# Nine token tiles regrouped from 3-3-3 to 2-3-4 in a fused encoder layer, with smaller rings beside them

## The reference

```python
h  = modulate(x, sh1, sc1)                       # layer norm, scale and shift from silu(c) @ w_ada
gq, gk, gv, glr, gog, sq, sk, sv, mg_a, mg_b = split_cols(h @ w_in)
# branch A: gated linear attention, 4 heads (dk 128, dv 256): S_t = diag(a_t) S_{t-1} + k_t v_t^T ; o_t = q_t S_t
branch_a = (rms_norm(o_gla) * gla_norm_w * silu(gog)) @ w_gla_proj
# branch B: stick breaking, 16 heads of 64: A[t,s] = sigmoid(z_ts) * prod_{s<j<t} (1 - sigmoid(z_tj))
branch_b = o_sb @ w_sb_proj
mix = (sigmoid(mg_a) * branch_a + sigmoid(mg_b) * branch_b) @ w_o
x   = layer_norm(DN_ALPHA * x + g1 * mix, ln1_w, ln1_b)
h2  = modulate(x, sh2, sc2)
# PEER: 8 heads; the 16 best of 128 keys on each of two sides, then the 16 best of their 256 sums
act = gelu(einsum('nhkd,nd->nhk', peer_u[eid], h2))      # 128 experts for each token
f   = einsum('nhk,nhkd->nd', softmax(top) * act, peer_v[eid])
x   = layer_norm(DN_ALPHA * x + g2 * f, ln2_w, ln2_b)
```

## Time and profile before

| | |
|---|---|
| runs shown | 4612.33, 4616.6, 4627.35 us |
| median | 4616.6 us |
| span of the profiled execution, first to last instruction | 4610.3 us |
| the median beside this span | 6.3 us more |
| busy PE, DVE, ACT, POOL | 76%, 59%, 20%, 53% of the span |
| moved by DMA | 1572.17 MB, 341 GB/s in the mean |

### The profile page before, as it was taken

The page is one execution under the profiler, slowest core; times in us unless marked ns, Lnnn a source line. Parts: engine busy times, 40 slices in busy tenths (PEclk is TensorE's granted clock), DMA queues, the critical chain, the costliest instruction groups (busy, mean ns, idle before and its releaser), DMA issues.

```text
span 4610.3 us, 46291 instructions
## 1 busy us (share of the span) xinstructions
PE 3486.6 (76%) x16122; PEld 1731.9 (38%) x16122; DVE 2734.5 (59%) x6463; ACT 911.3 (20%) x1858; POOL 2441.7 (53%) x2375
## 2 busy tenths in 40 slices
PE   7989999989899898978898988998443344433456
PEld 4656755655356443544443554434100000000011
DVE  3443412788876768775568757777843565575410
ACT  3552310134423100133444222001000000000000
POOL 0000000275777565567776766655666666666665
PEclk9999999999999899999999988998655555555567
DMA  7774452799999999999998999999999899999998
GB/s 305 285 263 191 163 164 82 277 328 329 347 377 374 384 419 400 407 351 378 391 387 321 375 358 406 407 403 393 374 378 379 336 372 377 374 370 352 375 372 316
DMA packets 422693, 1572.17 MB, mean 341 GB/s; under 512 B 47720, under 2 KB 63464, under 8 KB 411328
## 3 DMA queue, kind: packets, MB, share of 16 engines
q0 software_dynamic: 340384, 1289.90, 72.2%
q1 hardware_dynamic: 78448, 271.38, 15.8%
q10 hardware_dynamic: 3632, 7.94, 0.5%
HBM read 1526.42 MB, written 42.61 MB: 340 GB/s over the span
## 4 chain that ended last, share of the span: by engine, by line
PE 42%; DVE 18%; POOL 11%; another core or an unknown queue 10%; issue 9%; DMA 8%; ACT 1%; ACTq 0%; DVEq 0%; SPq 0%; POOLq 0%
PE bank L2606 7%; DVE peer_u_ring L2712 6%; PE wide L1891 6%; DMA peer_v_ring<-in_peer_v,expertsT 5%; POOL peer_u_ring L2539 4%; PE wide L1460 4%; PE wide L808 4%; POOL peer_v_ring L2549 4%; PE wide L2233 4%; PE wide L1448 3%; PE wide L871 2%; POOL w_ring L2549 2%; DMA peer_u_ring<-in_peer_u,experts 2%; PE wide L881 2%
## 5 line engine op out<-in xcount | busy, mean ns | idle before, releaser
L2539 POOL DMA_INDIRECT peer_u_ring<-in_peer_u,experts x1098 | 1153.2, 1050 | 603.0 <-issue 299.5
L2549 POOL DMA_INDIRECT peer_v_ring<-in_peer_v,expertsT x840 | 881.9, 1050 | 515.1 <-PE bank L2606 222.6
L2712 DVE SCALAR_TENSOR_TENSOR peer_u_ring<-peer_u_ring,wide 128x1024 f32<-128x1024 f32 x654 | 781.7, 1217 | 408.0 <-DMA peer_u_ring<-in_peer_u,experts 325.8
L2606 PE MATMUL bank<-peer_v_ring,peer_lone 128*32 128x512 f32 x3360 | 607.6, 730 | 450.3 <-DMA peer_v_ring<-in_peer_v,expertsT 280.9
L2606 PE MATMUL bank<-w_ring,peer_lone 128*32 128x512 f32 x1056 | 303.5, 962 | 345.7 <-DMA w_ring<-in_peer_v,expertsT 199.5
L2712 DVE SCALAR_TENSOR_TENSOR peer_u_ring<-peer_u_ring,peer_h 128x1024 f32<-128x1024 f32 x444 | 532.4, 1219 | 15.0 <-DMA peer_u_ring<-in_peer_u,experts 9.9
L2606 PEld LDWEIGHTS bank<-peer_v_ring,peer_lone 128*32 128x32 f32 x3360 | 92.8, 117 | 791.3 <-issue 771.9
L2549 POOL DMA_INDIRECT w_ring<-in_peer_v,expertsT x264 | 252.3, 956 | 141.2 <-issue 74.6
L808 PE MATMUL wide<-hT,w_ring 128*128 128x384 f32 x768 | 271.5, 501 | 6.9 <-ACT hT L589 3.6
L2606 PEld LDWEIGHTS bank<-w_ring,peer_lone 128*32 128x32 f32 x1056 | 50.5, 140 | 582.0 <-issue 576.6
L1460 PE MATMUL wide<-w_ring,hT 128*128 128x256 f32 x1152 | 260.4, 383 | 0.2 <-issue 0.2
(11 more groups left out here) (332 smaller groups left out, 5204.5 us busy)
## 6 DMA issues: line engine op xcount, KB each, us to landing
w_ring<-in_weights SPq DMA_DIRECT2D x312, 512.0 KB
sb_kc<-in_kcT POOLq DMA_DIRECT2D x16, 2048.0 KB, 7.7
sb_vc<-in_vc POOLq DMA_DIRECT2D x16, 2048.0 KB, 8.6
peer_u_ring<-in_peer_u,experts POOLq DMA_INDIRECT x1098
mod_w<-in_w_ada SPq DMA_DIRECT2D x15, 1024.0 KB, 10.8
peer_v_ring<-in_peer_v,expertsT POOLq DMA_INDIRECT x840
mod_w_later<-in_w_ada SPq DMA_DIRECT2D x9, 1024.0 KB, 7.0
scores<-sel_sc SPq DMA_DIRECT2D x6, 1024.0 KB
```

Of the source, the lines that this page charges most:

```text
L2539: pool.indirect_dma_start(buffer, None, K.A["peer_u"], bass.IndirectOffsetOnAxis(ap=K.ids_of[:, j % CHOSEN, k:k + 1], axis=0)).then_inc(lo ...
L2549: pool.indirect_dma_start(buffer, None, K.A["peer_v"], bass.IndirectOffsetOnAxis(ap=K.ids_of_turned[:, j % CHOSEN, t:t + 1], axis=0)).then ...
L2606: last = pe.matmul(self.F.psum[strip:strip + 32, :], self.lone[:, mark - at:mark - at + 32], self.buffer("v", m)[0][:, c * HALF:(c + 1) * ...
L2712: dve.scalar_tensor_tensor(u, u, 1.0, h2, ALU.mult, ALU.mult, accum_out=self.dots[:, j % 2, k:k + 1]).then_inc(self.dot_done, 1)
```

## The change

The groups become {0, samples}, {1, 2, 3}, {4, 5, 6, 7}. The u ring has six buffers instead of eight, there are two places for the chosen lists instead of four and one for the gates, and the buffers of the stages are laid out anew so that a group of four tiles fits. The first group has one prompt tile, so its stick stage has one key step per pair instead of two, and the order in `tensor_early`, `scalar_early` and `vector_early` loses the second step's calls. New waits guard the places that are used sooner again. The turned outputs of the GLA stage have two buffers only where they fit (first group); the banks of the selection follow the number of tiles. The causal masks of prompt and samples are two tensors now.

```diff
-NU, NV = 8, 6
+NU, NV = 6, 6
-CHOSEN = 4
+CHOSEN = 2
-GROUPS = grouped(((0, 2, True), (2, 5, False), (5, 8, False)))
+GROUPS = grouped(((0, 1, True), (1, 4, False), (4, 8, False)))
...
-            i, u = 2 * p, 2 * p
+            u = 2 * p
             self.c_scores(pe, G, u)
...
-            self.to_here(pe, G, i)
+            self.to_here(pe, G, p)
...
-            self.later_keys(pe, G, i)
-            self.scores(pe, G, i + 1)
             next(ahead, None)
-            self.values(pe, G, i)
+            self.values(pe, G, p)
             self.c_scores(pe, G, u + 1)
             next(ahead, None)
             self.c_turn(pe, G, u)
-            self.to_here(pe, G, i + 1)
...
+    def turned_slots(self, G):
+
+        return 2 if 2 * G.T <= max(g.T for g in GROUPS) else 1
...
-                if n == 0 and h >= 2:
-                    act.wait_ge(self.oT_out[h % 2], 16 * (2 * G.n + h // 2))
+                was = h - self.turned_slots(G)
+                if n == 0 and was >= 0:
+                    act.wait_ge(self.oT_out[was % 2], 16 * (2 * G.n + was // 2 + 1))
...
+        if j:
+            dve.wait_ge(self.K.peer.w_ready, j)
+        gates = self.K.gates[:, :].rearrange("p (h k) -> p h k", h=PEER_HEADS)
...
-    REFILL, MORE_FROM = 16, 5
-    TURN = SLOTS % (NU + NV)
+    REFILL, MORE_FROM = 16, 4
+    TURN = -SLOTS % NU
...
     def free_ids(self, dve, j):
         if j >= CHOSEN:
-            dve.wait_ge(self.v_used, P // 2 * (j - CHOSEN + 1))
+            dve.wait_ge(self.dot_done, SLOTS * (j - CHOSEN + 1))
```

More of the change, by code:

```diff
@@ L870, in to_here @@
             clears = kb == G.hi - 1 and (h == 0 or G.W > HALF // 2)
-            last = pe.matmul(r[:, h, c0:G.W], K.from_here[:, :], self.l[:, n % self.NL, h, c0:G.W], start=clears, stop=True, skip_group_check=True)
+            last = pe.matmul(r[:, h, c0:G.W], K.from_here[:, :], self.l[G.n][:, n % self.NL, h, c0:G.W], start=clears, stop=True, skip_group_check=True)
         last.then_inc(self.R.full, 1)
@@ L880, in later_keys @@
             for h in range(2):
-                last = pe.matmul(r[:, h, c0:G.W], K.before[:, :], self.l[:, n % self.NL, h, c0:G.W], start=False, stop=True, skip_group_check=True)
+                last = pe.matmul(r[:, h, c0:G.W], K.before[:, :], self.l[G.n][:, n % self.NL, h, c0:G.W], start=False, stop=True, skip_group_check=True)
             last.then_inc(self.l_used, 1)
@@ L1008, in tensor_early @@
             self.c_turn(pe, G, u)
-            self.to_here(pe, G, i + 1)
             next(ahead, None)
-            self.later_keys(pe, G, i + 1)
             self.c_values(pe, G, u)
-            next(ahead, None)
-            self.values(pe, G, i + 1)
             next(ahead, None)
@@ L1599, in key_scales @@
         m = self.prompt_tile(G, h, n)
-        if h or n >= 2:
-            at = self.tile(G, h, n - 2) if n >= 2 else self.tile(G, h - 1, G.np + n - 2)
+        had = h * G.np + n - 2
+        if had >= 0:
+            at = self.tile(G, *divmod(had, G.np))
             act.wait_ge(self.att_bank(at).full, self.att_bank(at).full_at["att", at])
@@ L1736, in hide_future @@
             dve.wait_ge(self.O.full, self.O.full_at["o", tile - 2])
-        dve.tensor_tensor(self.att[:, tile % 2, :], out[:, 0:P], self.K.causal[:, int(n == G.np), :], ALU.mult).then_inc(bank.kept, 1)
+        dve.tensor_tensor(self.att[:, tile % 2, :], out[:, 0:P], (self.K.causal_sample if n == G.np else self.K.causal)[:, :], ALU.mult).then_inc(bank.kept, 1)
     def next_state(self, dve, G, h, n):
@@ L1897, in scalar @@
         K = self.K
-        act.wait_ge(K.gla.oT_out[0], 16 * 2 * (G.n + 1))
+        for n in range(2):
+            act.wait_ge(K.gla.oT_out[n], 16 * 2 * (G.n + 1))
         for j in range(KC):
```

108 lines of the change are left out of this document (58 added, 50 removed).

## The result

| | before | after |
|---|---|---|
| median, us | 4619.65 (4 runs, 4612.33 to 4627.35) | 4871.35 (4 runs, 4864.29 to 4874.12) |
| profiled execution, span | 4610.3 | 4868.8 |
| ratio | | 1.053, interval 1.0498 to 1.0561 |

The changed kernel is slower by 5.3%. The forecast was 4830, in a range of 4715 to 4930.

A forecast was written before the change was run, and what follows sets the result against it. PE was taken to bound the middle, with DMA a close second, and gathers the tail. Front 726, second group 890, third 1505 and tail 1707 sum to 4828 us; with 6 carried over, rounded down, 4830, range 4715 to 4930.

The forecast's parts named there:

- its main term: Tail after the last stages: 530 dots instead of 402.5, 1707 us with the drain instead of 1345, so +362 us.
- That bytes do not bound the middle: Second and third groups' stages: PE is the floor, needing 1009 and 1224 us without value-row waits; DMA a close second.
- The tail is limited by the gathers: Tail: the gathers, not the choice of the next tile, limit it; a dot with its two gathers takes 2.84 us.
- A faster tail: Rival, in the tail: POOL's pace allows 2.49 us a slot, tail 190 us shorter, total 4640 us; chance 5%.
- (b) Rings: u ring of six instead of eight, POOL still six ahead: costs 0 us, ends -5 and +60.
- (c) Lists and single buffers: New waits name work 12 to 100 slots earlier: 0, ends 0 and +10; single turned GLA buffer 0, up to +5 a head.
- Front: First group's stages, 3 tiles to 2: 192 us less, ending at 726 us instead of 918.
- Second and third group, 890 and 1505: Lengths of the two later groups' stages: 890 us instead of 1073, and 1505 us instead of 1274.
- The ring starves both sides: Rival: PE stays at 88% in the middle (+137 us), a tail slot takes 3.0 us (+85), about 5050; chance 8%.
- DMA stays full, the shorter front is the gain: Rival: after the front the rings keep DMA full, so the end moves with the front to 4418 us; chance 4%.

The follow-up runs named there:

- 3-3-3: The kernel before the change, its tiles in three groups of three, with eight u buffers: 4619.65 us; with six u buffers instead, 4716.05 us.
- the runs with half rows: Each value gather brings 256 KB instead of 512, PE's work kept: 4598.18 us in the kernel before, 4843.58 us in the changed kernel.
- 2-3-4: The changed kernel's grouping, two, three and four tiles: 4871.35 us with six u buffers; 4791.64 us with eight, some small loads left out.
- the three runs: Changed kernel, front's stick stage: useless PE products added, 4834.21 us; sample pass's DVE scan cut to 64 columns, 4830.45 us; cache loads halved, 4835.58 us.

## Why the prediction was right, and where it was not

**The total and its main term: right.** The tail's 402.5 dots became 529, as forecast (530), for +383 us against +362. The slot is 2.885 instead of 2.84 us. The ring seems to have its part in these 0.045 us: in 3-3-3 the step from eight buffers to six made the tail 16 us longer, and in the changed kernel with eight a slot is again 1510 us / 530 dots = 2.85.

**That bytes do not bound the middle: right,** by the runs with half rows. That PE's own work is its floor fits, but was not shown. The worth that I gave to PE's waits for value rows was too high: 58 us of them went with half rows, and the middle was 6 us shorter.

**"The tail is limited by the gathers", with a slot set by DMA: right number, wrong limit.** In the rival *A faster tail* I wrote that it "would need the DMA to do better". With 25% fewer bytes to move the tail was no faster. POOL's pace plus its stalls is the limit as far as the profile shows, and the 2.49 us that I gave for POOL leaves the stalls out: they are 94 us in 402.5 slots, 0.23 us each, and the waits for dots are another 0.13, which with 2.49 make 2.85. The term came out right because the slot was measured and carried over, not derived.

**(b) Rings, "I take 0": the failed step.** Measured were 96 us in 3-3-3 and 40 to 70 in 2-3-4, about the upper end of 60 that I kept for it. The argument was that POOL needs 2.49 us a slot where 2.84 and more pass, so it catches up. But with six buffers POOL stood 218 us for dots in the third group of 3-3-3 where it had stood 89, and PE 100 us for values where it had waited 50. The reading that I give to this is that in the middle the dots do not come evenly, since DVE serves the stages too, and that POOL's one queue carries u and v gathers, so a wait for a dot holds values back as well. Averages over a slot do not see that. The other half of the argument, that longer slots make six buffers reach as far as seven, fits the smaller cost in 2-3-4, but no run tests it by itself.

**(c) Lists and single buffers, "0":** not tested alone. In the trace of the changed kernel the write that the single turned buffer could hold up (`gla_oT`, L1658) shows waits for PE only, 15.4 and 23.2 us in the two later groups, so nothing speaks against it.

**Front: mis-sized by 28 us, with the wrong reason.** The front ended at 754 us for 726. Merge (-47 for -52), output projection (-15 for -17) and norm (-2 for -3) held. GLA gave 71 instead of 57. The selection gave 7 instead of 15: at its end PE stands 19.2 us for the next group's norm on DVE, which is busy with the choice of the heads. Stick gave 22 instead of 48. I cut its gain for the sake of the cache loads, and these had air. As the three runs read, the removed key step had been cover for the sample pass's chain on ACT and DVE, and with PE waiting for that chain the granted clock is 0.83 where it was 0.95.

**Second and third group, 890 and 1505: met by two errors that cancel.** That is luck. The changed kernel with eight buffers, which is what these terms reckoned, shows 876 and 1460. Its idle times are 61 and 106 us, as predicted (57 and 110). PE's work is 815 and 1354 instead of 833 and 1395. I had carried over busy times of a middle at clock 0.94, and here it is 0.96 and 0.97. Taken at these clocks, my 833 and 1395 would be 816 and 1352, so this is about the whole difference. The ring then put back what the work had been overrated by. I had said that PE's waits for value rows would nearly vanish in the middle. In the third group 42.5 us stayed, and with eight buffers 21.8.

**The rivals.** *The ring starves both sides* was named and priced at 5050, but I gave it as all or nothing. The truth lies between: the ring is a sixth to two fifths of the loss of 252 us. *DMA stays full, the shorter front is the gain* is out: DMA was at 0.83 and 0.88 in the middle.

## What to carry to other kernels

Move work between stages by asking what will stand alone at the end: a tile that leaves a covered stretch for an uncovered one is paid in full, and one that is pushed into a covered stretch is free only as long as the engine there is fed. A ring cannot be judged by mean pace, nor by the consumer's waits on the page of one kernel; shrink it by itself and time it. A share of 0.95 for DMA is not yet a bound: take a quarter of the bytes away and look.

## What was not expected of the hardware

- In the tail, a 128-row gather keeps POOL for 0.94 + 0.30 us whether a row has 4 KB or 2 KB, and a 64-row gather for 0.90 + 0.30. Besides, POOL stalls there for up to 7 us at a time, some 28 times in 1143 us, with full rows and with half rows alike. What it waits for was not found.
- Gathers of 64 rows into partitions 0 to 63 brought the DMA share to 1.00 at 233 GB/s. The Trainium skill, "SBUF — State Buffer", section on the DMA port swizzle, says that DMA bandwidth goes by how many of the 16 ports the partitions reach; partitions 0 to 63 reach half of them. An estimate by that half of the ports is that 256 KB take what 512 KB take, and a pair of gathers no longer than before, 2.9 us. The run shows 3.4, so it agrees in the direction and not in the whole size.
- In the front's stick stage, useless work on PE in place of waits shortened the stage by 19 us, with the granted clock at 0.95 instead of 0.83. The gain was not kept to the end of the kernel.
